# HGRN tile ends re-ordered, gathers paced, one FFN sum moved, and attention's value product as channel by token with probabilities divided first

## The chip, the cores and the metric

The kernel runs on one core of one Trainium2 chip. The metric is the device time of one execution in microseconds. TensorE is called PE (its weight loads PEld), VectorE DVE, ScalarE ACT, GpSimd POOL and SyncE SP; PEclk is the share of full clock that TensorE was granted.

## The reference

One decoder layer in float32 for a prompt of 1024 tokens and 8 sample tokens, D = 1024.

```
h1 = LN(alpha*x + 0.5*SwiGLU(x));  m = attention heads | HGRN2 heads, then w_out
h2 = LN(alpha*h1 + m);             y = LN(alpha*h2 + 0.5*SwiGLU(h2))
attention: indexer picks top 256 causal keys a query; p = softmax(q k / 8), o = p v
HGRN2:     S_t = diag(f_t) S_{t-1} + (1-f_t) i_t^T,  o_t = S_t^T q_t, RMS norm, silu gate
```

For the prompt, the selection is a mask added to the scores of all keys up to the query's block, so attention is dense in work: 8 query blocks of 128, 8 heads of 64 channels, 2 key/value heads. The sample rows gather their 256 selected keys and values from paged caches.

## The kernel before

All five engines have their own written-out program, and semaphores order them. The stages are FFN 1 (0 to 985 us of the span), projections, indexer and threshold search (to 1253), HGRN (to 1658), prompt attention (to 1902), the sample rows (to 1986), w_out (to 2118) and FFN 2 (to the end).

**FFN.** Each pair of hidden tiles is a Strassen-like scheme of seven products for gate and for up, in the order 1, 2, 6, 7, 5, 3, 4 (`up_pair`, matmuls at L1531). POOL forms the weight sums for gate, DVE those for up: `up_sums(0, p+1)` is three operations of 128x512 (L1870 to L1873) for the next pair. DVE multiplies product 3 into `h12` (L1891, `hidden`); that frees the PSUM bank in which the up half of the next pair's product 1 starts.

**HGRN.** Four tiles of two heads. A tile has eight level passes: DVE makes scaled operands (`level`, L1195 to L1200), PE multiplies the halves of all 8 blocks (`level_products`, L651), and DVE merges the PSUM result by mask (`mask`, L1213). A level's products need the banks that the mask of the level before has read. Between them DVE runs one bit of the sample rows' threshold search in each `sample_slot`: compare, count on PE (`count`, L606), fix the bit (L1088). Projection units (`unit`, L527 for 344 columns, L532 for 256) lie beside the levels by the table BESIDE; AFTER holds three more for the next tile, put into the tile's end. That end is, in order: tail keys (L1265), turned by PE (L674), copied by ACT (L913), update products (L682), eight state steps (L1220), output products (L692 with the masked matrix, L694 with the state, alternating), squares and root on ACT (L917, L919), and `outputs` on DVE (L1226 to L1236). `keep_top` (L1161 to L1167) turns a threshold into a mask.

**Attention.** 64 steps (block, head), from 8 key blocks down to 1. PE forms the scores of two heads (`qk_pair`, L711), DVE adds the mask and finds the maximum (`biggest`, L1293, L1295), ACT takes the exponential with its sum (L929), PE turns the probabilities (`turn_probs`, L722), ACT copies them (L938), and PE multiplies them by the values (`pv`, L732) to token by channel. After 8 heads DVE divides by the sums (L1302, L1303), PE turns the block (L741), and ACT stores it (L943). Meanwhile POOL issues 32 indirect gathers for the sample rows (L468) one after another. SP loads w_out by `mix(14..17)` into ring slots 2, 3, 0, 1.

Of the kernel before, what the change touches and what calls it, by code (L numbers as in the profile page):

```python
# [9 lines left out]
def build_decoder_step(nc, I, O):  # L10
# [10 lines left out]
    P = 128  # L21
# [23 lines left out]
    with ctx:  # L45
# [157 lines left out]
        def score(b):  # L203
# [31 lines left out]
        PT = TMP[:, 2048:4096].rearrange("p (u c) -> p u c", c=1024)  # L235
        OTOK = AUX[:, 0:1024].rearrange("p (u c) -> p u c", c=512)
# [25 lines left out]
        RSUM = SMALL[:, 120:128]  # L262
# [36 lines left out]
        at_qk, at_sm, at_exp, at_tr, at_ptc, at_pv, at_on, at_ott, at_otc = (sem("at_" + x) for x in (  # L299
            "logits", "max", "exp", "turned", "pt", "pv", "normed", "out_turned", "out_copied"))  # L300
# [25 lines left out]
        for beside, spread in ((row_units("rg", 0) + gate_units(1, 0), (1, 1, 2, 2, 2, 2, 1, 1)),  # L326
                               (gate_units(2, 0) + ri1[5:], (0, 1, 1, 1, 1, 1, 1, 1)),
                               (row_units("rg", 1) + gate_units(3, 0), (1, 1, 2, 2, 2, 2, 1, 1)), ([], (0,) * 8)):
            u, levels = len(UNITS), []
            for n in spread:  # L330
                levels.append(list(range(u, u + n)))
                u += n
            assert u == len(UNITS) + len(beside)
            UNITS += beside
            BESIDE.append(levels)
            AFTER.append(list(range(u, u + 3)) if beside else [])
            if beside:
                UNITS += gate_units(len(BESIDE), 1)
# [53 lines left out]
        def pool_mixer(pool, G, link):  # L392
# [16 lines left out]
            with nc_ok:  # L409
# [56 lines left out]
                for j in range(16):  # L466
                    for name, dst in (("cache_k", KS), ("cache_v", VS)):
# [20 lines left out]
                for slot in (2, 3, 0, 1):  # L488
# [22 lines left out]
        def pe_mixer(pe, cols, mean, var):  # L511
# [142 lines left out]
            for t in range(4):  # L654
                for lv in range(NPASS):
                    level_products(t, lv)
                    if (t, lv, 0) in DEC_SLOTS:
                        count(DEC_SLOTS.index((t, lv, 0)))
                    if t == 3:
# [6 lines left out]
                    for i, u in enumerate(BESIDE[t][lv]):  # L666
                        unit(u)
                        if i == 0 and (t, lv, 1) in DEC_SLOTS:
                            count(DEC_SLOTS.index((t, lv, 1)))
                pe.wait_ge(h_kt, t + 1)  # L670
                pe.wait_ge(h_at, 12 * (t + 1))
                pe.wait_ge(h_ax, 4 * (t + 1))
# [3 lines left out]
                for u in AFTER[t][0:1]:  # L676
                    unit(u)
                pe.wait_ge(h_ktok, t + 1)
                for c in range(BLK):
                    for hd in range(2):  # L680
                        rows = slice(64 * hd, 64 * hd + 64)
                        last = M(PS[rows, 6, HD * c:HD * c + HD], KTOK[:, c, rows], RI[:, c, P * t + HD * hd:P * t + HD * hd + HD],  # L682
                                 start=True, stop=True)
                last.then_inc(h_u, 1)
                for c in range(BLK):
                    if c:
                        pe.wait_ge(h_state, BLK * t + c)
                    for hd in range(2):
                        rows = slice(64 * hd, 64 * hd + 64)
                        out = PS[:, 4 + hd, HD * c:HD * c + HD]  # L690
                        e0 = P * t + HD * hd
                        last = M(out, AT[:, hd, c, :], RI[:, c, e0:e0 + HD], start=True, stop=c == 0)  # L692
                        if c:
# [22 lines left out]
            def turn_probs(i):  # L716
                b, _ = STEPS[i]
                pe.wait_ge(at_exp, i + 1)
# [6 lines left out]
            def pv(i):  # L725
                b, h = STEPS[i]
                pe.wait_ge(at_ptc, i + 1)
                if h == 0 and i:
                    pe.wait_ge(at_on, i // H)
                for j in range(b + 1):  # L730
                    c = P + HD * (h // 4)
                    last = M(PS[:, 2, HD * h:HD * h + HD], PT[:, i % 2, P * j:P * j + P], KV[:, j, c:c + HD],  # L732
                             start=j == 0, stop=j == b)
                last.then_inc(at_pv, 1)

            def turn_out_rows(bi):
                pe.wait_ge(at_on, bi + 1)
                if bi:
                    pe.wait_ge(at_otc, bi)
                for j in range(4):  # L740
                    last = T(PS[:, 3, P * j:P * j + P], OTOK[:, bi % 2, P * j:P * j + P], IDENT[:, :])  # L741
                last.then_inc(at_ott, 1)
# [9 lines left out]
            pv(63)  # L752
            turn_out_rows(7)


# [70 lines left out]
        def act_mixer(act, A, link, square, sd, gain):  # L826
# [79 lines left out]
            for t in range(4):  # L906
# [7 lines left out]
                for u in AFTER[t][0:1]:  # L914
                    unit(u)
                act.wait_ge(h_o, t + 1)
                A(OSQ.rearrange("p (u c) -> p u c", u=2), PS[:, 4:6, :], ACT.Square).then_inc(h_osq, 1)  # L917
                act.wait_ge(h_ss, t + 1)
                A(SR, SS, ACT.Sqrt, scale=1.0 / HD, bias=EPS[:, 2:3]).then_inc(h_sd, 1)  # L919
                for u in AFTER[t][1:3]:  # L920
                    unit(u)

            def expo(i):
                b, h = STEPS[i]
                act.wait_ge(at_sm, i + 1)
                if h == 0 and i >= 2 * H:
                    act.wait_ge(at_on, i // H - 1)
# [4 lines left out]
            def copy(i):  # L932
# [3 lines left out]
                if i >= 2:  # L936
                    act.wait_ge(at_pv, i - 1)
                A(PT[:, i % 2, 0:n], PS[:, 0:2, :].rearrange("p u c -> p (u c)")[:, 0:n], ACT.Copy).then_inc(at_ptc, 1)  # L938

# [1162 lines left out]
```

## Time and profile before

| what | us |
|---|---|
| median of 3 runs (lowest, highest) | 2991.72 (2990.32, 2992.75) |
| the profiled execution | 3020.13 |
| its span, first to last instruction | 3018.4 |
| mean granted clock | 0.934 |

The profiled execution is 28.4 us (0.95%) above the median; 1.7 us of its time lie outside the span. In a window's row the numbers in brackets are instruction counts. In a timeline the bracket at the end is the idle time of that engine before the instruction and who ended it; "issue" and "remote" are waits for which the profile shows no releaser. A float32 matmul appears as two PE instructions.

### The profile page before, as it was taken

To read this page: it belongs to the slowest core of one execution; us is meant where nothing else is said; L and a number is where in the kernel's file an instruction comes from. 1 tells how busy PE (TensorE), PEld (TensorE's weight loads), DVE (VectorE), ACT (ScalarE), POOL (GpSimd) and SP (SyncE) were. 2 spreads that over 40 slices of the span, in tenths; PEclk is the share of its full clock that TensorE was granted. 3 is DMA by queue.
4 is the path that set the end of the run, shared out by engine and by line. 5 is a ranking of instruction groups with operands and counts; after the bars stand their busy time and mean duration, and the time that the engine had idled before them with its cause. 6 is when DMAs were issued, how large, how long until landed. Compare 5 with 4: busy or idle time off the path is not lost.

```text
span 3018.4 us, 42478 instructions
## 1 busy us (share of the span) xinstructions
PE 2725.2 (90%) x17013; PEld 2440.3 (81%) x17013; DVE 1599.4 (53%) x3027; ACT 653.5 (22%) x1497; POOL 552.0 (18%) x534
## 2 busy tenths in 40 slices
PE   7999999999999799997996688398799999999996
PEld 7999999999987478875765566255799999999996
DVE  5654565365421878866668232413555455446543
ACT  1110221022011656410110344101221022102112
POOL 4321231133010111000000300212222132122300
PEclk9999999999999999988996787589899999999998
DMA  6473464346421233100100010101356246524632
GB/s 169 121 180 78 112 160 122 96 112 169 114 85 43 49 102 91 43 1 1 29 1 5 25 56 1 42 1 42 80 134 157 77 130 160 132 75 128 155 98 74
DMA packets 444179, 260.63 MB, mean 86 GB/s; under 512 B 8968, under 2 KB 436120, under 8 KB 443984
## 3 DMA queue, kind: packets, MB, share of 16 engines
q1 hardware_dynamic: 435712, 234.22, 29.5%
q0 software_dynamic: 8272, 23.70, 2.8%
q8 instruction: 136, 2.23, 0.3%
q14 instruction: 59, 0.48, 0.1%
HBM read 251.07 MB, written 6.81 MB: 85 GB/s over the span
## 4 chain that ended last, share of the span: by engine, by line
PE 63%; DVE 17%; issue 14%; ACT 3%; POOL 1%; SPq 1%; DMA 1%; DVEq 0%; POOLq 0%; ACTq 0%
PE ps L1531 22%; PE ps L1595 18%; PE ps L527 7%; PE ps L818 4%; PE ps L532 4%; DVE big L1870 3%; PE ps L651 2%; PE ps L592 2%; DVE big L1873 1%; DVE down_weights L1046 1%; PE ps L692 1%; PE ps L694 1%; DVE weight_ring L1887 1%; PE ps L583 1%; ACT acts L1713 1%
## 5 line engine op out<-in xcount | busy, mean ns | idle before, releaser
L1531 PE MATMUL ps<-aux,big 128*128 128x172 f32 x2112 | 339.5, 315 | 37.1 <-ACT big L1726 35.7
L1887 DVE TENSOR_TENSOR weight_ring<-ps,big 128x172 f32<-128x172 f32 x396 | 123.8, 331 | 440.9 <-ACT big L1726 393.3
L1531 PEld LDWEIGHTS ps<-aux,big 128*128 128x128 f32 x2112 | 320.7, 194 | 44.6 <-ACT big L1726 40.7
L1531 PE MATMUL ps<-acts,weight_ring 128*128 128x172 f32 x2112 | 333.2, 311 | 22.4 <-DVE weight_ring L1891 20.3
L1531 PEld LDWEIGHTS ps<-acts,weight_ring 128*128 128x128 f32 x2112 | 311.2, 190 | 37.1 <-issue 36.7
L1531 PE MATMUL ps<-weight_ring 128*128 128x172 f32 x2112 | 329.7, 309 | 0.0
L1531 PEld LDWEIGHTS ps<-weight_ring 128*128 128x128 f32 x2112 | 314.2, 190 | 0.0
L1595 PE MATMUL ps<-big 128*128 128x172 f32 x1584 | 238.8, 309 | 0.0
L527 PE MATMUL ps<-acts,weight_ring 128*128 128x344 f32 x768 | 238.2, 467 | 0.0
L1595 PEld LDWEIGHTS ps<-big 128*128 128x128 f32 x1584 | 233.1, 190 | 0.0
L2031 POOL TENSOR_TENSOR big<-weight_ring 128x512 f32<-128x512 f32 x66 | 83.8, 1269 | 726.6 <-PE ps L1531 702.9
L1726 ACT ACTIVATE big<-ps 128x172 f32<-128x172 f32 x396 | 119.4, 310 | 440.1 <-PE ps L1531 440.1
L527 PEld LDWEIGHTS ps<-acts,weight_ring 128*128 128x128 f32 x768 | 148.4, 197 | 73.9 <-issue 7.2
L532 PE MATMUL ps<-weight_ring,acts 128*128 128x256 f32 (+3 forms) x864 | 180.3, 364 | 0.0
L1730 ACT ACTIVATE weight_ring<-weight_ring 128x172 f32<-128x172 f32 x198 | 68.0, 344 | 478.3 <-DVE weight_ring L1887 478.2
L1531 PE MATMUL ps<-acts,big 128*128 128x172 f32 x1056 | 164.9, 309 | 0.0
L532 PEld LDWEIGHTS ps<-weight_ring,acts 128*128 128x128 f32 (+1 forms) x864 | 142.3, 180 | 25.9 <-issue 1.3
L1948 DVE SCALAR_TENSOR_TENSOR acts<-acts,ps 128x172 f32<-128x172 f32 x96 | 31.7, 330 | 247.3 <-PE ps L1595 247.3
L1595 PE MATMUL ps<-big,weight_ring 128*128 128x172 f32 x1056 | 159.9, 309 | 0.0
L1595 PE MATMUL ps<-big,down_weights 128*128 128x172 f32 x1056 | 159.9, 309 | 0.0
L1531 PEld LDWEIGHTS ps<-acts,big 128*128 128x128 f32 x1056 | 157.2, 190 | 0.0
L1595 PEld LDWEIGHTS ps<-big,down_weights 128*128 128x128 f32 x1056 | 155.6, 190 | 0.0
(335 smaller groups left out, 3932.1 us busy)
## 6 DMA issues: line engine op xcount, KB each, us to landing
weight_ring<-ffn_wg SPq DMA_DIRECT2D x132, 512.0 KB, 5.3
weight_ring<-ffn_wu SPq DMA_DIRECT2D x132, 512.0 KB, 7.0
down_weights<-ffn_wd SPq DMA_DIRECT2D x24, 1408.0 KB, 11.6
weight_ring<-ffn_wd SPq DMA_DIRECT2D x24, 1408.0 KB, 9.8
weight_ring<-w_in SPq DMA_DIRECT2D x9, 1024.0 KB, 5.3
weight_ring<-w_in SPq DMA_DIRECT2D x8, 512.0 KB, 7.2
weight_ring<-w_out SPq DMA_DIRECT2D x4, 1024.0 KB, 11.7
out_y_prompt<-weight_ring SPq DMA_DIRECT2D x8, 512.0 KB, 2.6
```

The costliest lines, as they stand in the source:

```text
L527: last = M(PS[:, u % 3, 0:TW], w[:, k, P * a:P * a + P], ACTS[:, k, cols(x)], start=k == 0, stop=k == DT - 1)
L532: last = M(PS[0:rows, u % 3, 0:a], ACTS[:, k, P * x:P * x + rows], w[:, k, :], start=k == 0, stop=k == DT - 1)
L592: last = M(PS[:, 5 + r % 2, 32 * j:32 * j + 32], KXT[:, r % 2, P * j:P * j + P], QB[:, :, :, 2 * gp:2 * gp + 2], start=True, stop=True)
L651: last = M(PS[:, 4 + 2 * half + hd, P * (c % 4):P * (c % 4) + P], k, q, start=True, stop=True)
L818: last = M(PS[:, y % 6, 0:TW], w[:, k, P * (d % 2):P * (d % 2) + P], src, start=k == 0, stop=k == DT - 1)
L1531: last = M(PS[:, 3 * m + bank, 0:QW], lhs[:, i, :], rhs[:, i, :], start=begin and i == 0, stop=end and i == KH - 1, skip_group_check=True)
L1595: last = M(PS[:, x + bank, 0:QW], lhs[:, i, :], rhs[:, i, :], start=begin and i == 0, stop=end and i == LAST, skip_group_check=True)
L1726: A(ST[:, m, c, :], PS[:, 3 * m, 0:QW], ACT.Copy).then_inc(cp_done, 1)
L1730: A(CG[:, i, :], CG[:, i, :], ACT.Silu).then_inc(sl_done, 1)
L1870: V.tensor_tensor(s1, a21, a22, ALU.add).then_inc(su_done[1], 1)
L1887: V.tensor_tensor((CG, CU)[m][:, (out, i)[m], :], PS[:, 3 * m + bank, 0:QW], ST[:, m, part, :], ALU.add)\
L2031: G.tensor_tensor(s1, a21, a22, ALU.add).then_inc(su_done[0], 1)
```

## The change

The diff does six things. FFN: `up_sums(0, p+1)` stands after `h12`. HGRN: BESIDE units go into the first six levels, AFTER units into levels 5 and 6; the counts stand ahead of the level's products and ahead of the units; the output products with the masked matrix run before the update products, into banks 6 and 7; `gates`, `queries` and the next tile's first `level` go ahead of `keep_top` and `outputs` on DVE, and the second half of the next tile's first products waits for `outputs`. Gathers wait for three attention steps a pair. Attention: every step's probabilities are divided ahead of turning (`normalise(i)`), and `pv_pair` multiplies values (stationary, 64 columns) by turned probabilities of two heads, so the result needs no turning. w_out loads in the order slot 0, 1, 2, 3, the last after attention.

```diff
-        for beside, spread in ((row_units("rg", 0) + gate_units(1, 0), (1, 1, 2, 2, 2, 2, 1, 1)),
-                               (gate_units(2, 0) + ri1[5:], (0, 1, 1, 1, 1, 1, 1, 1)),
-                               (row_units("rg", 1) + gate_units(3, 0), (1, 1, 2, 2, 2, 2, 1, 1)), ([], (0,) * 8)):
+        for beside, spread in ((row_units("rg", 0) + gate_units(1, 0), (2, 2, 2, 2, 2, 2, 0, 0)),
+                               (gate_units(2, 0) + ri1[5:], (1, 1, 1, 1, 1, 2, 0, 0)),
+                               (row_units("rg", 1) + gate_units(3, 0), (2, 2, 2, 2, 2, 2, 0, 0)), ([], (0,) * 8)):
...
                 for j in range(16):
+                    if j:
+                        pool.wait_ge(at_exp, 3 * j)
...
-                for slot in (2, 3, 0, 1):
+                for slot in range(4):
...
                     if t:
-                        pe.wait_ge(h_orow, t)
+                        pe.wait_ge(h_state, BLK * t)
...
+                    elif t and half:
+                        pe.wait_ge(h_orow, t)
...
-                    level_products(t, lv)
                     if (t, lv, 0) in DEC_SLOTS:
                         count(DEC_SLOTS.index((t, lv, 0)))
+                    level_products(t, lv)
+                    if (t, lv, 1) in DEC_SLOTS:
+                        count(DEC_SLOTS.index((t, lv, 1)))
...
+                    if lv == 5:
+                        for u in AFTER[t][0:1]:
+                            unit(u)
+                    elif lv == 6:
+                        for u in AFTER[t][1:3]:
+                            unit(u)
...
-                for u in AFTER[t][0:1]:
-                    unit(u)
+                pe.wait_ge(h_at, 12 * (t + 1))
+                pe.wait_ge(h_ax, 4 * (t + 1))
+                for c in range(BLK):
+                    for hd in range(2):
+                        e0 = P * t + HD * hd
+                        M(out(hd, c), AT[:, hd, c, :], RI[:, c, e0:e0 + HD], start=c == 0, stop=True, skip_group_check=True)
                 pe.wait_ge(h_ktok, t + 1)
...
+                for c in range(1, BLK):
+                    pe.wait_ge(h_state, BLK * t + c)
                     for hd in range(2):
-                        last = M(out, AT[:, hd, c, :], RI[:, c, e0:e0 + HD], start=True, stop=c == 0)
-                        if c:
-                            last = M(out, LV[rows, (t + 1) % 2, P * c:P * c + P], SC[rows, c, :], start=False, stop=True)
+                        last = M(out(hd, c), LV[rows, (t + 1) % 2, P * c:P * c + P], SC[rows, c, :],
+                                 start=False, stop=True, skip_group_check=True)
                 last.then_inc(h_o, 1)
-                for u in AFTER[t][1:3]:
-                    unit(u)
...
-                pe.wait_ge(at_exp, i + 1)
+                pe.wait_ge(at_sc, i + 1)
...
+            def pv_pair(q):
+                b, h = STEPS[2 * q]
+                bi = q // 4
+                pe.wait_ge(at_ptc, 2 * q + 2)
+                if q % 4 == 0 and bi >= 2:
+                    pe.wait_ge(at_otc, bi - 1)
+                c = P + HD * (h // 4)
                 for j in range(b + 1):
+                    for e in range(2):
+                        last = M(PS[64 * e:64 * e + 64, 2 + bi % 2, P * (q % 4):P * (q % 4) + P], KV[:, j, c:c + HD],
+                                 PT[(2 * q + e) % 4][:, P * j:P * j + P], start=j == 0, stop=j == b)
...
             for i in range(64):
                 turn_probs(i)
-                if i:
-                    pv(i - 1)
+                if i % 2 == 0 and i:
+                    pv_pair(i // 2 - 1)
                 if i % 2 == 0 and i + 2 < 64:
                     qk_pair(i // 2 + 1)
-                if i >= H and i % H == 2:
-                    turn_out_rows(i // H - 1)
...
             def queries(t):
+                V.tensor_copy(PF, HF[:, 0:SEQ]).then_inc(hf_free, 1)
...
+                if t < 3:
+                    gates(t + 1)
                 states(t)
                 if t < 3:
-                    gates(t + 1)
+                    queries(t + 1)
+                    level(t + 1, 1)
...
                 outputs(t)
-                if t < 3:
-                    queries(t + 1)
-                    level(t + 1, 1)
...
+            def normalise(i):
+                n = P * (STEPS[i][0] + 1)
+                dve.wait_ge(at_exp, i + 1)
+                r = RSUM[:, i % 2:i % 2 + 1]
+                link(V.reciprocal(r, SUMS[:, (i // H) % 2, i % H:i % H + 1]))
+                s = SM[:, i % 2, 0:n]
+                V.tensor_scalar(s, s, r, None, ALU.mult).then_inc(at_sc, 1)
+            biggest(0)
             for i in range(64):
-                biggest(i)
-                if i and i % H == 0:
-                    normalise(i // H - 1)
+                if i + 1 < 64:
+                    biggest(i + 1)
+                normalise(i)
...
+                elif m == 15:
+                    sp.wait_ge(at_pv, 32)
...
-                    for m in range(2, len(MIX)):
+                    for m in [*range(2, 14), 16, 17, 14, 15]:
...
-                if j < LAST:
-                    up_sums(0, p + 1)
                 dve.wait_ge(up_mm, up_count(p, 3, 1))
                 dve.wait_ge(sl_done, 4 * p + 3)
                 hidden(h12, h12, PS[:, 3, 0:QW])
+                if j < LAST:
+                    up_sums(0, p + 1)
```

PT now has four buffers, two of them in ring slot 3; `out_rows` copies the product's bank as it is.

## Rows read from the trace of the kernel before

**Rows 1.** The page's chain that ended last: share of the span by engine.
```profile
PE 63%; DVE 17%; issue 14%; ACT 3%; POOL 1%; SPq 1%; DMA 1%; DVEq 0%; POOLq 0%; ACTq 0%
```
**Rows 2.** Windows: length, busy time of PE, PEld, DVE, ACT, POOL, PEclk, DMA share, GB/s.
```profile
1253.00:1658.00 405.00, 340.46 (x2170) 268.75 (x2170) 282.49 (x538) 47.19 (x85) 10.61 (x13) 0.84 0.03 7
1365.00:1438.00 73.00, 53.43 (x366) 44.30 (x363) 54.30 (x105) 5.61 (x13) 0.00 (x0) 0.81 0.00 1
1658.00:1902.00 244.00, 194.20 (x1093) 153.41 (x1094) 78.63 (x234) 94.84 (x200) 28.79 (x30) 0.74 0.09 26
```
**Rows 3.** What L1531 waited for: us in total, times.
```profile
  DVE weight_ring L1891: 20.3, 59
```
**Rows 4.** Timeline of one FFN pair: start us, us, engine line, what, times [idle <-releaser].
```profile
321.59 1.75 DVE L1870 TENSOR_TENSOR big<-weight_ring 128x512 f32<-128x512 f32 x1
...
325.55 0.32 DVE L1891 TENSOR_TENSOR weight_ring<-weight_ring,ps 128x172 f32<-128x172 f32 x1
...
325.98 3.51 PEld L1531 LDWEIGHTS ps<-acts,weight_ring 128*128 128x128 f32 x24 [0.53 <-issue]
```
**Rows 5.** Waits from 1253 to 1658, DVE: us in total, times, longest.
```profile
DVE rejected L1088 <- PE ps L606: 34.4, 16, 4.0
```
**Rows 6.** Timeline of tile 0: one level's products; the tile's end.
```profile
1280.87 2.25 PE L651 MATMUL ps<-weight_ring 64*128 64x128 f32 x32 [1.40 <-DVE aux L1213]
...
1334.99 1.15 PE L682 MATMUL ps<-big,weight_ring 128*64 128x64 f32 x32
...
1352.10 11.52 PE L527 MATMUL ps<-acts,weight_ring 128*128 128x344 f32 x32
...
1364.37 2.06 PE L651 MATMUL ps<-big 64*128 64x128 f32 x32 [0.75 <-DVE down_weights L1182]
```
**Rows 7.** Timeline of tile 1's end on DVE: `keep_top`, then `outputs`.
```profile
1454.32 1.27 DVE L1161 TENSOR_SCALAR_CACHE_REDUCE big<-down_weights,candidate 128x1024 uint8<-128x1024 f32 x1
...
1455.63 0.75 DVE L1162 TENSOR_SCALAR weight_ring<-down_weights,candidate 128x1024 f32<-128x1024 f32 x1
...
1464.50 1.22 DVE L1226 TENSOR_REDUCE small<-weight_ring 128x16 f32<-128x1024 f32 x1 [2.23 <-ACT weight_ring L917]
1467.71 1.29 DVE L1236 TENSOR_TENSOR big<-big,ps 128x512 f32<-128x512 f32 x2
```
**Rows 8.** Timeline, attention with 1024 keys: `pv` at 0.5; then two steps at 1.0.
```profile
1702.19 3.52 PE L732 MATMUL ps<-big,weight_ring 128*128 128x64 f32 x16
...
1709.29 0.30 PEld L711 LDWEIGHTS ps<-big 64*128 64x128 f32 x4
1711.20 1.09 PE L722 MATMUL ps<-ident,weight_ring 128*128 128x128 f32 x8
...
1712.14 1.90 PE L732 MATMUL ps<-big,weight_ring 128*128 128x64 f32 x16
...
1712.69 1.23 DVE L1293 CUSTOM_DVE_ANT_0 weight_ring<-ps,down_weights 128x1024 f32<-128x1024 f32 x1
1713.96 0.15 DVE L1295 TENSOR_SCALAR small<-small 128x1 f32<-128x1 f32 x1
...
1717.78 1.77 PE L711 MATMUL ps<-big 64*128 64x512 f32 x8
```
**Rows 9.** Forms in attention: busy us, mean ns | idle before, releasers.
```profile
L1302 DVE RECIPROCAL small<-small 128x8 f32<-128x8 f32 x8 | 1.6, 203 | 27.2 <-PE ps L732 27.2
```
**Rows 10.** Timeline while the gathers run.
```profile
1677.37 1.02 ACT L938 ACTIVATE weight_ring<-ps 128x1024 f32<-128x1024 f32 x1 [4.27 <-remote]
...
1693.77 1.00 POOL L468 DMA_INDIRECT big<-cache_v,gather_rows  x1 [0.30 <-issue]
1698.54 1.02 ACT L938 ACTIVATE weight_ring<-ps 128x1024 f32<-128x1024 f32 x1 [18.36 <-remote]
```
**Rows 11.** Window of attention's last 50 us, columns as rows 2.
```profile
1850.00:1900.00 50.00, 43.77 (x186) 35.12 (x185) 13.49 (x66) 19.81 (x67) 0.00 (x0) 0.50 0.00 0
```
**Rows 12.** Timeline after attention: the path to the sample rows.
```profile
1915.50 3.50 DVE L1324 TENSOR_TENSOR down_weights<-big,down_weights 128x512 f32<-128x512 f32 x1 [15.09 <-DMA big<-scratch_ri]
```

More of the change, by code:

```diff
@@ L234, in build_decoder_step @@
         SM = TMP[:, 0:2048].rearrange("p (u c) -> p u c", c=1024)
-        PT = TMP[:, 2048:4096].rearrange("p (u c) -> p u c", c=1024)
-        OTOK = AUX[:, 0:1024].rearrange("p (u c) -> p u c", c=512)
+        PT = [TMP[:, 2048 + 1024 * i:3072 + 1024 * i] for i in range(2)] + [RING[:, 3, 1024 * i:1024 * i + 1024] for i in range(2)]
         KS = BIG[:, 2 * C4:2 * C4 + 2048].rearrange("p (j c) -> p j c", c=P)
@@ L261, in build_decoder_step @@
         SUMS = SMALL[:, 104:120].rearrange("p (u h) -> p u h", h=H)
-        RSUM = SMALL[:, 120:128]
+        RSUM = SMALL[:, 120:122]
         SS, SR = SMALL[:, 128:144], SMALL[:, 144:160]
@@ L298, in build_decoder_step @@
         kvout = sem("kv_out")
-        at_qk, at_sm, at_exp, at_tr, at_ptc, at_pv, at_on, at_ott, at_otc = (sem("at_" + x) for x in (
-            "logits", "max", "exp", "turned", "pt", "pv", "normed", "out_turned", "out_copied"))
+        at_qk, at_sm, at_exp, at_sc, at_tr, at_ptc, at_pv, at_otc = (sem("at_" + x) for x in (
+            "logits", "max", "exp", "normed", "turned", "pt", "pv", "out_copied"))
         qd_zero, qd_in, vn_in, s0_in, vb_in = sem("qd_zeroed"), sem("qd_in"), sem("vn_in"), sem("s0_in"), sem("vb_in")
@@ L665, in pe_mixer @@
                             select_c(lv - 4)
-                    for i, u in enumerate(BESIDE[t][lv]):
+                    for u in BESIDE[t][lv]:
                         unit(u)
-                        if i == 0 and (t, lv, 1) in DEC_SLOTS:
-                            count(DEC_SLOTS.index((t, lv, 1)))
+                    if lv == 5:
[4 more added lines that the diff above has]
+                            unit(u)
                 pe.wait_ge(h_kt, t + 1)
-                pe.wait_ge(h_at, 12 * (t + 1))
-                pe.wait_ge(h_ax, 4 * (t + 1))
+                pe.wait_ge(h_ax, 4 * t + 3)
                 for c in range(BLK):
@@ L681, in pe_mixer @@
                         rows = slice(64 * hd, 64 * hd + 64)
-                        last = M(PS[rows, 6, HD * c:HD * c + HD], KTOK[:, c, rows], RI[:, c, P * t + HD * hd:P * t + HD * hd + HD],
+                        last = M(PS[rows, 4, HD * c:HD * c + HD], KTOK[:, c, rows], RI[:, c, P * t + HD * hd:P * t + HD * hd + HD],
                                  start=True, stop=True)
                 last.then_inc(h_u, 1)
-                for c in range(BLK):
-                    if c:
-                        pe.wait_ge(h_state, BLK * t + c)
+                for c in range(1, BLK):
+                    pe.wait_ge(h_state, BLK * t + c)
                     for hd in range(2):
                         rows = slice(64 * hd, 64 * hd + 64)
-                        out = PS[:, 4 + hd, HD * c:HD * c + HD]
-                        e0 = P * t + HD * hd
-                        last = M(out, AT[:, hd, c, :], RI[:, c, e0:e0 + HD], start=True, stop=c == 0)
-                        if c:
-                            last = M(out, LV[rows, (t + 1) % 2, P * c:P * c + P], SC[rows, c, :], start=False, stop=True)
+                        last = M(out(hd, c), LV[rows, (t + 1) % 2, P * c:P * c + P], SC[rows, c, :],
+                                 start=False, stop=True, skip_group_check=True)
                 last.then_inc(h_o, 1)
-                for u in AFTER[t][1:3]:
-                    unit(u)
             pe.wait_ge(h_orow, 4)
@@ L913, in act_mixer @@
                 A(KTOK[:, :, :].rearrange("p (u c) x -> p u (c x)", u=2), PS[:, 4:6, :], ACT.Copy).then_inc(h_ktok, 1)
-                for u in AFTER[t][0:1]:
+                for u in AFTER[t]:
                     unit(u)
                 act.wait_ge(h_o, t + 1)
-                A(OSQ.rearrange("p (u c) -> p u c", u=2), PS[:, 4:6, :], ACT.Square).then_inc(h_osq, 1)
+                A(OSQ.rearrange("p (u c) -> p u c", u=2), PS[:, 6:8, :], ACT.Square).then_inc(h_osq, 1)
                 act.wait_ge(h_ss, t + 1)
                 A(SR, SS, ACT.Sqrt, scale=1.0 / HD, bias=EPS[:, 2:3]).then_inc(h_sd, 1)
-                for u in AFTER[t][1:3]:
-                    unit(u)
             def expo(i):
@@ L925, in expo @@
                 act.wait_ge(at_sm, i + 1)
-                if h == 0 and i >= 2 * H:
-                    act.wait_ge(at_on, i // H - 1)
+                if i >= 2 * H:
+                    act.wait_ge(at_sc, i - 2 * H + 1)
                 s = SM[:, i % 2, 0:P * (b + 1)]
@@ L948, in act_mixer @@
                 copy(i)
-                if i >= H and i % H == 2:
+                if i >= H and i % H == 1:
                     out_rows(i // H - 1)
@@ L1235, in outputs @@
                 for hd in range(2):
-                    last = V.tensor_tensor(rg[:, hd], rg[:, hd], PS[:, 4 + hd, :].rearrange("p (c e) -> p c e", e=HD), ALU.mult)
+                    last = V.tensor_tensor(rg[:, hd], rg[:, hd], PS[:, 6 + hd, :].rearrange("p (c e) -> p c e", e=HD), ALU.mult)
                 last.then_inc(h_orow, 1)
```

46 lines of the change are left out of this document (11 added, 35 removed).

## The prediction

> **What bounds the kernel now.** I read the chain that ended last, then windows by stage, then waits and timelines at the six places that the diff touches. PE carries 63% of the chain and DVE 17% [rows 1]. In both FFNs PE is the bound, so what counts there is its idle time. HGRN and attention are hand-offs between PE and DVE: HGRN's 405 us hold 340 of PE and 282 of DVE, attention's 244 hold 194 and 79 [rows 2]. Their clock is 0.84 and 0.74 of full, so the level granted matters as much as the instruction count. The reader should see that PE's 194 busy microseconds in attention are no proof that PE work sets its length.
>
> The sum goes by the profiled execution, 3020.13 us, 28.4 above the median of 2991.72. I carry the difference over unchanged and treat the one place where that is doubtful (the gathers) apart.
>
> **FFN: up_sums behind h12.** PE waits for L1891 59 times [rows 3]. In the timeline the three sums begin at 321.59, h12 ends only at 325.87, and PE's load resumes at 325.98 after 0.53 us idle [rows 4]. With h12 first it is done about 0.35 us after product 3, some 3 us before its bank is needed, so the wait goes: 59 x 0.55 = **-32 us**. What is late next? The sums start about 0.8 us later, at 322.4, and with 4.0 us (325.55 - 321.59) end near 326.4; their reader, product 6 of the next pair, stands behind the 24 loads that end at 329.5 (325.98 + 3.51). The addition and SiLU behind them slip 0.6 us, with over 1 us to spare. Bounds: 0, if another engine is late at once, and -35.
>
> **HGRN.** Per tile the mixed output products run from 1336.14, the end of L682, to 1352.10: 16.0 us [rows 6]. Apart they are 32 instructions like L732's, 1.90/16 = 0.12 us each [rows 8], 3.8 us, and 28 of 64 columns, at most 0.11 each by L651's 2.25/32 = 0.07 and what is left for waits on the states, 3.1 us. That is 9 less a tile, 36 in all. Here the row is first: one block's share is 16.0/8 = 2.0 us for seven or eight instructions of 0.12. [...]
>
> The counts ahead of the level's products take from DVE's 34.4 us of waiting [rows 5]. In tiles 0 and 2, with two units beside each level, PE becomes the bound, and the second count now holds the units until DVE's compare; I take 11 of the 34.
>
> Against this stands a new wait. The second half of the next tile's first products waits for `outputs`, and PE has nothing behind it that may pass. On DVE stand before that: queries and a level (3.7 us, six operations of about 0.65), `keep_top` (1464.50 - 2.23 - 1454.32 = 8.0 us, not in tile 0), and `outputs` with its ACT steps (1464.50 to 1469.00, 4.5 us) [rows 7]. PE idles 8 + 16 + 15 = 39 us in three tile ends, where before it had units: 11.5 us of L527 directly behind the outputs [rows 6]. The units are not gone but moved into the levels, where only tile 1 has room: 73.0 - 53.4 = 20 us idle [rows 2], of which I let 12 take them up. Sum: -36 - 11 + 39 - 12 = **-20 us**; bounds -40 (the idle covered) and +10 (units make all levels longer).
>
> **Attention, the chain of a pair.** Before, with 1024 keys at full clock, a pair of heads takes 1717.78 - 1709.29 = 8.49 us [rows 8]. On PE it is two turnings of 0.86 (1.09 with the drain), two value products of 1.87 and the scores of 1.8: 7.3 of 8.5, mostly hidden behind DVE and ACT and they behind it. After the change the order in the code is a strict alternation: `biggest(2q+2)` needs the scores; `normalise(2q+1)` stands behind it on DVE; turning 2q+1 needs that; `biggest(2q+3)` needs this turning (its buffer); then `normalise(2q+2)`, turning 2q+2, `pv_pair`, and the next scores. Prices: `biggest` 1712.69 to 1714.11 = 1.42; `normalise` a reciprocal of 0.20 [rows 9] and a scaling like L1162's 0.75 of the same 1024 columns [rows 7], 1.0 with the gap; turnings 1.09 and 0.86; `pv_pair` has no row. Bounds: it has 32 instructions of 128 columns, of pairs on different column halves. L651's pairs of row halves with the same 128 columns take 0.07 each; L682's pairs of column halves with 64 columns 1.15/32 = 0.036 [rows 6]; alone they would take L732's 0.12. So 1.7 to 3.8 us; I take 2.0, next to L682, which is the same layout. Sum: 2 x 1.42 + 2 x 1.0 + 1.09 + 0.86 + 2.0 + 1.8 + four hand-offs of 0.05 = 10.8 us, **2.3 more than before**, although PE lost 1.7 us of work. Most pieces shrink with the key blocks; I let the difference fall evenly to 0.2 at one block, a mean of 1.25, times 32 pairs: +40. Off go the division at the block ends (27.2 us of DVE waits in eight [rows 9], of which 11 are on the chain, as the pair around a block end is some 3 longer while scores fill all four banks), `keep_top` now beside more PE work (-3) and the last division and turning (-2). [...] At an equal clock: **+27 us**.
>
> **Attention, the clock.** PE's needed time falls to 5.6 of 10.8 us. [...] `pv` at the lower level took 3.52 instead of 1.90 [rows 8]. If all pairs of three or more key blocks ran low, each would lose its PE pieces once more: 5.6 us at eight blocks, 2.1 at three, a mean of 3.9 over 24, 93 us. I take **+26**: three tenths more of the time low than before. Bounds 0 and +65. [...]
>
> **Gathers.** From 1673.1 to 1677.4 and from 1680.2 to 1698.5 ACT stood still with all it needed done, and moved 4 us after the last gather was issued [rows 10]: 22.6 us, 19 net of the value products that crept along. Three steps (some 13 us) between pairs of gathers leave room, and the last pair, after step 45, is early enough for the sample rows. But the profiled execution is above the timed ones by about this much (28.4 us), so whether those stall too is open. I take half: **-10 us**; bounds 0 and -22.
>
> **w_out and the tail.** Slot 3 holds probabilities until the end and loads only then, 1 MB beside the state loads that DVE waits for until 1915.50 [rows 12]: **+1 us**, bounds 0 and +6. The wait at POOL's scaling has 70 us of cover.
>
> **Sum.** -32 - 20 + 27 + 26 - 10 + 1 = -8 us: 3012 for a profiled execution, **2984 us** for the median. 0.2% (6 us) is what a measurement of this kernel tells from no change.
>
> **The rivals.**
> 1. Recovery: the stall is real in timed runs and the clock no worse. -32 - 20 + 27 + 3 - 19 + 1 = -40: 2952 us. For it: the standstill with all inputs ready. Against: PE's thinner work.
> [...]
> 3. The value pairs do not run side by side: 3.8 instead of 2.0 us at eight blocks, 32 us over all: 3016 us. Against: L682's 0.036.
> 4. The FFN gap stays, because another engine is late (the change doesn't do what it says): 3016 us. Against: only pairs with the sums ahead show it.
>
> **How the numbers follow.** Forecast 0.40 (2966 to 3000), rival 1 0.22, rival 2 0.24, rivals 3 and 4 0.07 each. The range is 2946 to 3026. Faster by over 0.2% (under 2985.7): 0.24 of the forecast, 0.22 of rival 1, 0.01 of the rest: 0.47. Within: 0.15. Slower: 0.38.
>
> **What would show it.** In the FFN: no wait for L1891. In HGRN: the masked products in one run of about 4 us; an idle of 8 to 16 us before the second half of the first products of tiles 1 to 3. In attention: pairs of 10.8 us at full clock with 1024 keys, the scaling following `biggest`, PEclk under 0.74, no standstill at the start. Wrong it is if pairs stay at 8.5 us or if attention's clock rises.

## The result, and the profile after

The changed kernel took 3021.87 us (median of 4, 3020.73 to 3023.45) against 2991.02 us for the kernel before (median of 4, 2989.20 to 2992.75): a ratio of 1.0104, 95% interval 1.0086 to 1.0121. It is 30.9 us, or 1.0%, slower. The forecast was 2984 us, a little faster than before; 3021.87 lies inside the range given, but the time moved the other way. The rival nearest to it is the second, which has 60 us for the lower clock in attention and nothing at the gathers: -32 - 20 + 27 + 60 + 1 = +36, 3028 us.

The profiled executions differ by 2 us only (3020.13 before, 3022.25 after). That is because the one of before stands still at the gathers [rows 10] and its timed runs in this comparison are 29 us shorter, which suggests that they did not. In the changed kernel the profiled execution and the timed median lie 0.4 us apart. The experiments come back to that.

The chain that ended last, after, beside rows 1: "issue" fell from 14% to 6%, and PE now has 74%.

```profile
PE 74%; DVE 16%; issue 6%; ACT 2%; DMA 1%; SPq 1%; POOL 1%; DVEq 0%; ACTq 0%; POOLq 0%
```

Windows of HGRN, of attention, and of attention's last 50 us, after (columns as in rows 2):

```profile
1245.00:1624.00 379.00, 290.49 (x2172) 234.62 (x2172) 282.14 (x533) 46.06 (x84) 8.84 (x11) 0.88 0.04 13
1624.00:1913.00 289.00, 178.32 (x1058) 118.23 (x1059) 110.49 (x346) 100.47 (x200) 30.96 (x31) 0.69 0.04 11
1863.00:1913.00 50.00, 29.54 (x139) 16.07 (x140) 17.11 (x90) 17.88 (x58) 0.00 (x0) 0.50 0.00 1
```

HGRN was 405 us [rows 2] and is 379. Attention was 244, of which 22.6 were the standstill [rows 10], and is 289: 45 us longer although it no longer stands still. DVE's time in it rose from 79 to 110 us, and the granted clock fell from 0.74 to 0.69. PE's 178.3 and DVE's 110.5 us add up to 288.8 of the 289: the two hardly ever work at the same time.

What PE waited for, in us, times and longest wait, over the whole span, after:

```profile
PE ps L731 <- DVE weight_ring L1302: 110.3, 63, 3.9
PE ps L1530 <- ACT big L1725: 39.1, 18, 11.7
PE ps L654 <- DVE big L1235: 32.0, 3, 13.9
...
PE ps L654 <- DVE aux L1212: 18.6, 8, 5.5
```

The first row is the new one in attention: 63 of the 64 turnings wait for the scaling (L1302), 1.75 us each. The third is the new one in HGRN, three tile ends, as predicted. The wait of the FFN's products for h12 [rows 3] has no row any more. One FFN pair, after (start us, us, engine, line): h12 is the first line, the sums for the next pair begin behind it at 317.80.

```profile
317.54 0.33 DVE L1890 TENSOR_TENSOR weight_ring<-weight_ring,ps 128x172 f32<-128x172 f32 x1 [0.58 <-PE ps L1530]
317.80 0.85 DVE L1869 TENSOR_TENSOR big<-weight_ring 128x512 f32<-128x512 f32 x1
...
319.82 4.68 PE L1530 MATMUL ps<-acts,weight_ring 128*128 128x172 f32 x31
```

PE runs through where rows 4 show its loads resuming at 325.98 after h12. The end of HGRN's tile 0, after, to hold against rows 6:

```profile
1331.75 3.69 PE L692 MATMUL ps<-big,aux 128*128 128x64 f32 x32
...
1336.90 2.34 PE L704 MATMUL ps<-big,weight_ring 64*128 64x64 f32 x28 [0.39 <-DVE big L1219]
...
1340.05 1.16 PE L654 MATMUL ps<-big 64*128 64x128 f32 x16 [0.81 <-DVE down_weights L1181]
...
1347.12 2.08 PE L654 MATMUL ps<-big 64*128 64x128 f32 x16 [5.90 <-DVE big L1235]
```

The masked products take 3.69 us in one run and the state products 2.34, together 6.0 where the mixed loop took 16.0. Then PE does half of the next tile's first products and waits 5.90 us for `outputs`.

The trace of before shows what the mixed loop was made of. PE alternates between two instructions of L692 and two of L694, with no wait for a state among them. In tile 0 such a group starts every 0.36 us at first, and every 0.62 us from 1339.15 on, where the granted clock is 0.50 although PE's records fill the window (the second excerpt, columns as in rows 2):

```profile
1337.33 0.43 PE L692 MATMUL ps<-big,aux 128*128 128x64 f32 x2
1337.70 0.43 PE L694 MATMUL ps<-big,weight_ring 64*128 64x64 f32 x2
...
1339.77 0.69 PE L692 MATMUL ps<-big,aux 128*128 128x64 f32 x2
1340.38 0.69 PE L694 MATMUL ps<-big,weight_ring 64*128 64x64 f32 x2
```

```profile
1339.00:1352.00 13.00, 13.00 (x44) 10.56 (x43) 2.17 (x5) 0.00 (x0) 0.68 (x1) 0.50 0.01 3
```

The four tiles took 16.0, 14.0, 15.0 and 15.9 us. With all 27 alternations at the full clock each would be 10.7 us (an estimate: 0.87 for the first six instructions and 27 x 0.364). So about half of what the new order saves is the alternation itself (10.7 - 6.0 = 4.7 us a tile) and half is the lower clock that went with it (15.2 - 10.7 = 4.5, with the mean of the four).

The same view of one pair of heads in attention, 1024 keys, after. It is the central piece of the result:

```profile
1664.22 1.23 DVE L1292 CUSTOM_DVE_ANT_0 weight_ring<-ps,down_weights 128x1024 f32<-128x1024 f32 x1 [2.32 <-PE ps L720]
...
1665.75 0.75 DVE L1302 TENSOR_SCALAR weight_ring<-weight_ring,small 128x1024 f32<-128x1024 f32 x1
...
1666.56 1.09 PE L731 MATMUL ps<-ident,weight_ring 128*128 128x128 f32 x8 [2.47 <-DVE weight_ring L1302]
...
1667.80 1.23 DVE L1292 CUSTOM_DVE_ANT_0 weight_ring<-ps,down_weights 128x1024 f32<-128x1024 f32 x1 [1.30 <-PE ps L731]
...
1670.14 1.97 PE L731 MATMUL ps<-ident,weight_ring 128*128 128x128 f32 x8 [2.48 <-DVE weight_ring L1302]
...
1672.04 3.68 PE L743 MATMUL ps<-weight_ring,big 128*64 128x128 f32 x32
...
1675.64 1.89 PE L720 MATMUL ps<-big 64*128 64x512 f32 x8
...
1677.57 1.09 DVE L1292 CUSTOM_DVE_ANT_0 weight_ring<-ps,down_weights 128x896 f32<-128x896 f32 x1 [7.49 <-PE ps L720]
```

The reader is to see a relay: `biggest`, scaling, turning, `biggest`, scaling, turning, value products, scores, and then `biggest` again after 7.49 us of waiting, with PE and DVE never beside each other. The order is the one that the prediction read from the code. It takes 13.35 us (1664.22 to 1677.57) where before it took 8.49 [rows 8]. PE's pieces come at two speeds: the first turning takes 1.09 us with 1.0 granted, the second 1.97 and the value products 3.68 with 0.5 granted.

### The profile page after: what moved, and what is told of

Read it like the earlier page. It is cut to its first block, busy times and chain, and to the rows that moved or that the text cites. A ratio compares the mean times of both kernels' runs of the same rounds, so it can differ in the third digit from the quotient of the medians.

```text
span 3020.4 us, 42557 instructions
## 1 busy us (share of the span) xinstructions
PE 2654.6 (88%) x16981; PEld 2381.9 (79%) x16981; DVE 1581.1 (52%) x3139; ACT 657.5 (22%) x1497; POOL 550.7 (18%) x534
## 4 chain that ended last, share of the span: by engine, by line
PE 74%; DVE 16%; issue 6%; ACT 2%; DMA 1%; SPq 1%; POOL 1%; DVEq 0%; ACTq 0%; POOLq 0%
PE ps L1530 29%; PE ps L1594 18%; PE ps L528 7%; PE ps L533 5%; PE ps L818 4%; PE ps L731 2%; PE ps L593 2%; PE ps L743 2%; PE ps L720 1%; DVE weight_ring L1292 1%; DVE down_weights L1044 1%; PE ps L584 1%; ACT acts L1712 1%; DVE weight_ring L1302 1%; PE ps L654 1%
## 5 line engine op out<-in xcount | busy, mean ns | idle before, releaser
L1530 PE MATMUL ps<-aux,big 128*128 128x172 f32 x2112 | 346.8, 319 | 42.5 <-ACT big L1725 39.1
L1530 PEld LDWEIGHTS ps<-aux,big 128*128 128x128 f32 x2112 | 326.8, 197 | 49.7 <-ACT big L1725 44.1
L1530 PE MATMUL ps<-acts,weight_ring 128*128 128x172 f32 x2112 | 319.2, 309 | 1.7 <-DVE acts L1816 0.9
L528 PE MATMUL ps<-acts,weight_ring 128*128 128x344 f32 x768 | 231.7, 458 | 0.0
L731 PE MATMUL ps<-ident,weight_ring 128*128 128x128 f32 x288 | 66.2, 378 | 110.3 <-DVE weight_ring L1302 110.3
```

The costliest lines, as they stand in the source:

```text
L528: last = M(PS[:, u % 3, 0:TW], w[:, k, P * a:P * a + P], ACTS[:, k, cols(x)], start=k == 0, stop=k == DT - 1)
L731: last = T(PS[:, j // 4, P * (j % 4):P * (j % 4) + P], SM[:, i % 2, P * j:P * j + P], IDENT[:, :])
L1530: last = M(PS[:, 3 * m + bank, 0:QW], lhs[:, i, :], rhs[:, i, :], start=begin and i == 0, stop=end and i == KH - 1, skip_group_check=True)
```

## The experiments

The kernel before did not stand still on every occasion. Kernels timed on the same occasion share its runs, so each comparison below has its own figure for it: 3014.49 us (3001.09 to 3020.81), 3014.83 (3003.30 to 3020.03), 2987.17 (2985.41 to 2990.42) and 3013.00 (2997.53 to 3021.04).

**e_ffn**: the kernel before with the FFN's edit alone, the last hunk of the diff.

> The kernel before with the FFN edit alone (up_sums behind h12), against 2991.0 us of before. Theory A (the gap is worth what PE itself idles, 0.30 us as PE's row has it, not the 0.53 of the loads' row; 58 pairs): -17 us, 2974. Theory B (the prediction's 0.55 us a pair): -32 us, 2959. If another engine is late at once: 2991.

Measured: 2995.61 us against 3014.49, ratio 0.9935 (0.9912 to 0.9958): -18.9 us (-13 to -27). The size is theory A's; the absolute time is not, because the kernel before stood at 3014. Between the two traces 6.1 of the 21.9 us lie in attention's first seven blocks (216.3 us, 222.3 before), whose code is the same in both, and 15.8 outside them.

**e_hgrn**: the HGRN edits alone (the spreads, the counts ahead of the products, the split output products, the bank change, gates and level moved).

> The kernel before with the HGRN edits alone. Theory A (the stage's 404 us in the trace of before and 379 in the trace of after is what the edits do): -25 us, 2966, with two to three idles of 6 to 14 us before the second half of the next tile's first products. Prediction: -20, 2971. Rival: the stage gains but the attention behind it starts at a lower clock and gives half of it back: 2979.

Measured: 2983.43 us, 0.9898 (0.9878 to 0.9919): -31.1 us. More than any of the three; e_ffnhgrn and h_again below come back to it.

**e_gather**: the wait ahead of each pair of gathers alone.

```
                 for j in range(16):
+                    if j:
+                        pool.wait_ge(at_exp, 3 * j)
```

> The kernel before with the paced gathers alone. Theory A (the standstill of 22.6 us is of the profiled execution only, which is 28 us above the timed ones): timed 2991 +- 3, its profiled execution about 2995 to 3000. Theory B (the timed runs stall too): 2970, profiled 2998.

Measured: 2992.62 us (2984.15 to 2999.55), 0.993 (0.9906 to 0.9955): -21.9 us. In the timeline of ACT in e_ffn, whose gathers are issued in one go, the standstill is there; it is the idle in brackets:

```profile
1674.13 1.02 ACT L938 ACTIVATE weight_ring<-ps 128x1024 f32<-128x1024 f32 x1 [7.45 <-remote]
...
1693.35 1.02 ACT L938 ACTIVATE weight_ring<-ps 128x1024 f32<-128x1024 f32 x1 [16.41 <-remote]
```

23.9 us in all. What ACT waited for in e_gather over the same stretch has no such row, and the copy (L940 there) waits 0.7:

```profile
ACT weight_ring L931 <- DVE small L1297: 26.8, 6, 7.1
ACT weight_ring L940 <- PE ps L724: 0.7, 1, 0.7
```

So the standstill is the gathers', and timed runs can have it (theory B on this occasion). It is seen in the profiled executions; for the timed ones it is inferred from the medians.

**e_noattn**: the three parts together, with the old attention and the old order of the w_out loads.

> The kernel before with the FFN, HGRN and gather edits and the old attention (and the old order of the w_out loads). Theory A (parts add): 2991 - 17 - 25 = 2949, and the attention part alone then costs 3022 - 2949 = +73 us. Rival (the parts interact, as the clock of one stage depends on the one before): 2960 to 2975.

Measured: 2944.36 us (2943.84 to 2945.94), 0.9773 (0.9750 to 0.9795). The three single gains sum to -71.8 us and this is -70.1: they add. Against the changed kernel it leaves 77.5 us for the attention part, the order of the w_out loads included, which was not tried alone.

**a_again**: the changed kernel once more.

> The changed kernel once more, to stand beside the kernel before where that runs 3001 to 3021 us. Theory A (the standstill at the gathers comes and goes with the occasion, in whole sets of runs, and only kernels that issue the gathers in one go have it): 3022 here too, however before stands. Rival (the occasion shifts all kernels alike): 3045.

Measured: 3021.65 us (12 runs, 3020.03 to 3023.79) against 3014.83, 1.0026 (1.0013 to 1.0039). Theory A: the changed kernel is where it was to 0.2 us, and the kernel before is 24 us up. The loss is 31 us where the kernel before runs free and 7 us where it stands still.

**e_swap**: the changed kernel with two statements of PE's loop exchanged.

```
+                if i % 2 == 0 and i + 2 < 64:
+                    qk_pair(i // 2 + 1)
                 if i % 2 == 0 and i:
                     pv_pair(i // 2 - 1)
-                if i % 2 == 0 and i + 2 < 64:
-                    qk_pair(i // 2 + 1)
```

> The changed kernel with the next pair's scores issued ahead of the pair's value products. Theory S (series: the value products stand between the turning and the next scores and DVE waits for both; 1.9 to 3.7 us a pair with 1024 keys, a mean of about 1.5): -48 us, 2974. Rival C (clock: DVE's and PE's alternation leaves PE too thin; the order within PE's stretch changes nothing in that): at most the half of it, 2998 and a clock in attention no higher.

Measured: 2960.34 us (2957.58 to 2963.30), 61.3 under a_again. More than theory S gave, and the clock rose, against C (0.78 in attention, 222 us instead of 289). The timeline shows what it does: scores (3.36 us at the lower clock, 0.50, where they took 1.89), then values, and DVE starts beside the values:

```profile
1665.33 1.97 PE L731 MATMUL ps<-ident,weight_ring 128*128 128x128 f32 x8 [2.48 <-DVE weight_ring L1302]
...
1667.23 3.36 PE L720 MATMUL ps<-big 64*128 64x512 f32 x8
...
1670.52 1.73 PE L743 MATMUL ps<-weight_ring,big 128*64 128x128 f32 x26
1670.62 1.09 DVE L1292 CUSTOM_DVE_ANT_0 weight_ring<-ps,down_weights 128x896 f32<-128x896 f32 x1 [5.34 <-PE ps L720]
```

**e_fill**: the changed kernel with work on PE whose result nobody reads, in the time in which it waits for the scaling.

```
-                pe.wait_ge(at_sc, i + 1)
                 if i:
                     pe.wait_ge(at_ptc, i)
+                for j in range(b + 1):
+                    T(PS[:, 0, 0:P], IDENT[:, :], IDENT[:, :])
+                pe.wait_ge(at_sc, i + 1)
```

> The changed kernel with idle work on PE: before each turning, once its bank is free and while the scaling is awaited, as many further turnings of the identity as there are key blocks. Theory C (at least 40 of the 76 us that attention lost are PE at the lower level because it idles): granted clock in attention from 0.69 to 0.85 or more, 2982 us. Theory S (the series is what costs; clock little): the clock may rise, the time stays at 3015 to 3030.

Measured: 2986.48 us (2985.48 to 2988.41): 35.2 us faster for 288 more instructions, with the clock in attention at 0.87 and its length 248 us. Theory C, though the gain is some 5 us short of the 40 that it named. The pair with 1024 keys, now at full clock throughout (1.00 from 1657.48 to 1668.12):

```profile
1657.48 1.23 DVE L1294 CUSTOM_DVE_ANT_0 weight_ring<-ps,down_weights 128x1024 f32<-128x1024 f32 x1 [0.74 <-PE ps L720]
...
1664.42 1.97 PE L745 MATMUL ps<-weight_ring,big 128*64 128x128 f32 x32
...
1668.12 1.09 DVE L1294 CUSTOM_DVE_ANT_0 weight_ring<-ps,down_weights 128x896 f32<-128x896 f32 x1 [4.78 <-PE ps L720]
```

10.64 us from one `biggest` to the next pair's (1668.12 - 1657.48), where the prediction had 10.8; the value products 1.97, where it had 2.0.

**e_nodiv**: the changed kernel without the scaling; the attention output is left undivided.

> The changed kernel without the scaling of the probabilities (the attention output is left undivided; the reciprocal stays). Theory S (the scaling of 0.75 us with 1024 keys, a mean of 0.52, stands in series 64 times): -35 us, 2987. Rival (PE is the bound and the scaling hides): 3020. If the clock rises with PE's idle time gone: down to 2970.

Measured: 2963.65 us (2954.39 to 2967.53), 58.0 under a_again, for a group of 33.3 us of DVE work. Its clock in attention is 0.77 instead of 0.69: with a piece of DVE work gone from the relay PE is without work for 75 of 231 us instead of 111 of 289, its clock is higher, and the gain is larger than the piece. The runs spread over 13 us, so the size is rough.

**e_swapfill** and **e_swapfill5**: both edits together; in the second, at least five idle turnings.

> The changed kernel with both the scores ahead of the value products (which gave -61 us alone) and the idle work ahead of each turning (-35 alone). If the two costs are separate (series and clock) and the order took only part of the clock's share: attention from 222 us to about 205, 2943. If the order already took what the idle work gives: 2960, or more where the idle work now delays PE.

> As the run before, with at least five idle turnings ahead of each (only pairs of four key blocks or fewer differ). If the lower clock of the last three blocks (0.50 to 0.82) is due to PE's idle time there: 5 to 10 us under that run. If the extra work lies in the way: 5 us above it.

Measured: 2942.33 us (2936.24 to 2945.95) and 2939.20 (2936.80 to 2939.65). The first is as expected if the costs are separate. The second is 3.1 us under it; its clock in the last query block, of one key block, is 1.00 where the first's is 0.73, but the ranges overlap.

**e_oldfill**: the old attention, otherwise as e_noattn, with the same idle turnings.

> The old attention with the FFN, HGRN and gather edits (2944 us) and the same idle work ahead of its turnings. Where PE at the lower level costs as much there as in the changed attention: 2925. As its turnings wait only 25 us for the exponential and its clock in attention is 0.86 already: at most -8, 2936 to 2944, and above 2944 if the idle work delays the turnings.

Measured: 2952.17 us (2951.31 to 2952.93), 7.8 above e_noattn (of another occasion) though its clock rose from 0.86 to 0.91. There the idle work lies in the way.

**e_ffnhgrn**: FFN and HGRN edits, gathers as before.

> The kernel before with the FFN and HGRN edits and the gathers as they were. If the gathers in one go cost 22 us whatever the rest: 2966, with a standstill of about 22 us in its trace. If the HGRN and FFN gains were partly the standstill shortened: 2950.

Measured: 2948.46 us (2946.12 to 2951.79), 0.9866 (0.9851 to 0.9881), against a kernel before of 2987.17. Neither expectation fits its own reason: nobody stood still on this occasion, the kernel before included, and this one's trace has no such wait. FFN and HGRN are worth 38.7 us there; with e_ffn's 18.9, which is from another occasion, that leaves 19.8 for HGRN.

**best**, **n_again**, **e_fill12**, **h_again**: the kernel of e_swapfill5, that of e_noattn and that of e_hgrn once more, and the changed kernel with twelve and eight idle turnings at every block.

> The whole change with the scores ahead of the value products and at least five idle turnings ahead of each turning. It gave 2939.2 beside another occasion's 2944.4 of the old attention. Theory (at a full clock the two attentions are level: 204 us here, 210 there): 2937 to 2941, 3 to 7 us under n_again.

> The FFN, HGRN and gather edits with the old attention once more: 2944, as before, whatever the occasion, since its gathers are paced.

> The changed kernel with more idle work: twelve idle turnings ahead of each even one and eight ahead of each odd one, at every block. If with e_fill's 0.87 clock there were still some 15 us to be had: clock in attention 0.95 or more, 2970 us, so that the clock costs about 50 of the 77 us and the series about 27. If the rest is series: 2986 or, with the idle work in the way at few key blocks, up to 3000.

> The kernel before with the HGRN edits alone, once more. If this occasion's kernel before runs without the standstill (2987 to 2991): -20 to -25 us, 2966 to 2970. If it stands still again: -31, 2983, and the five microseconds above come from a shorter standstill.

Measured: 2938.15 us (2936.41 to 2940.47), 2943.67 (2942.23 to 2946.28), 2983.04 (2982.57 to 2983.84) and 2981.03 (2980.35 to 2982.69). Attention in the first three, one window each, in the order e_fill12, n_again, best:

```profile
1628.00:1872.00 244.00, 198.59 (x1698) 152.14 (x1697) 110.22 (x346) 101.41 (x202) 31.47 (x32) 0.98 0.05 14
```

```profile
1625.00:1835.00 210.00, 168.89 (x1086) 134.68 (x1087) 78.47 (x234) 94.75 (x201) 30.77 (x32) 0.86 0.10 30
```

```profile
1625.00:1829.00 204.00, 165.77 (x1422) 117.52 (x1422) 110.56 (x346) 100.73 (x200) 31.43 (x31) 0.99 0.05 16
```

At 0.98 the changed attention still takes 244 us against the old one's 210 at 0.86. So of the 78.0 us between the changed kernel and n_again, the idle work brings back 38.6 (3021.65 - 2983.04) with the clock, and 39.4 stay: 34 in attention, 3 ahead of it and 2 behind. It falls between the two expectations of e_fill12.

That is no comparison at an equal clock, since the old attention is at 0.86. Other traces have single blocks of the same code at the full clock. The query block of four key blocks (four pairs of heads) in n_again and in e_gather, then three key blocks in n_again and in e_oldfill (idle work included), columns as in rows 2:

```profile
1753.72:1777.95 24.23, 19.66 (x122) 15.41 (x123) 7.56 (x27) 11.09 (x25) 5.87 (x6) 0.86 0.05 14
```

```profile
1794.44:1815.59 21.15, 16.58 (x122) 13.08 (x123) 7.56 (x27) 10.98 (x25) 5.87 (x6) 1.00 0.06 16
```

```profile
1777.95:1800.85 22.90, 20.03 (x98) 15.75 (x99) 6.52 (x26) 9.40 (x25) 4.64 (x6) 0.67 0.05 15
```

```profile
1787.92:1806.96 19.04, 15.96 (x123) 13.15 (x124) 6.52 (x27) 9.37 (x25) 4.55 (x5) 1.00 0.07 19
```

So n_again itself loses at least 7 us to the clock (3.1 and 3.9). At an equal clock the changed attention is then about 40 us longer than the old one and not 34, and about 32 of the 38.6 are what it loses to the clock beyond the old one. Both are estimates: the idle work may itself delay the blocks with few keys (four key blocks take 28.13 us in e_fill12 and 26.75 in e_fill, both at 1.00).

**best** beats the changed kernel by 83 us, the kernel before by 2.4% (ratio 0.9761, 0.9739 to 0.9784) where that stands still, and the old attention of n_again by 5.5 us, with ranges that do not meet. Against a kernel before that runs free the same kernel, as e_swapfill5, is 1.6% faster (0.9835, 0.9822 to 0.9849).

h_again stood still again (its first eight steps' stretch is 20 us longer than n_again's), as did the kernel before it was compared with. So its -32 us do not come from a shorter standstill, against what was expected. The attention behind the standstill took 173 us there and 183 in e_gather, two kernels with the same attention code (the kernel before's profiled execution has 182 from its ninth step on):

```profile
1691.00:1864.00 173.00, 139.54 (x899) 112.92 (x898) 62.23 (x202) 77.91 (x177) 0.00 (x0) 0.85 0.08 25
```

```profile
1693.00:1876.00 183.00, 152.93 (x904) 124.00 (x903) 62.37 (x202) 78.18 (x178) 26.78 (x28) 0.77 0.11 33
```

DVE and ACT do the same (62 and 78 us), PE's clock is 0.85 and 0.77. That is 9 to 10 of the 12 us between h_again and HGRN's 19.8. It does not go with the HGRN edits alone: e_ffn has the old HGRN, and its blocks of seven to two key blocks take 156.7 us as in h_again, against 164.8 in e_gather. What sets the level in one and not in the other was not tested.

## Why the prediction was wrong, point by point

- **FFN, -32 forecast, -18.9 measured.** The mechanism was right, the wait is gone. The mis-sized term is "59 x 0.55 = **-32 us**". It took the 0.53 us of idle time of PE's weight loads [rows 4] for PE's own; rows 3 had the total for PE's matmuls, 20.3 us in 59 times, 0.34 each. In e_ffn two other waits of PE grew, the ones for ACT L1726 from 35.7 to 38.7 us and for DVE L1832 from 28.4 to 29.9: 20.3 - 4.5 = 15.8. Of the fourth rival only these 4.5 us came true.
- **HGRN, -20 forecast, -19.8 measured** on an occasion without standstill, and -25 between the traces. The total is right, its terms less so. The output products save 37 us in the four tiles where 36 was said, but the 16.0 us of tile 0 were the longest of the four, and about half of the saving is the lower clock that the alternation ran at (0.50), which the prediction does not count. The new idle is 32.0 us in three tile ends (5.9, 13.9 and 12.2) where 39 was. The counts did not give 11: DVE's wait for them is 38.9 us in twelve (L1086) against 34.4 in sixteen [rows 5]. What makes up for it is the level's shorter wait (PE for DVE, 41.0 us before and 18.6 after). That the total fits so well is partly luck.
- **Attention at an equal clock, +27 forecast, about +40 measured** (at least +34, e_fill12 against n_again). This is the first step that failed. The order and the pair's 10.8 us at 1024 keys were right (10.64). What failed is "I let the difference fall evenly to 0.2 at one block". From a block's first `biggest` to the next block's, e_fill12 is 4.7, 3.9, 9.0, 5.6, 3.9, 1.4 and 3.6 us longer than n_again for eight to two key blocks, and 7.0 and 5.3 for four and three by the rows at the full clock. The forecast, with its 13 us of savings spread evenly, has 7.6, 6.4, 5.2, 4.0, 2.8, 1.6 and 0.4: too much for many keys, too little for few. Why the loss does not shrink with the keys was not tested. The terms named come to 40 - 11 - 3 - 2 = 24; the other 3 of the 27 are a guess of 0.1 us a pair for one more change between shapes of product, which no run shows. What the traces show of such changes is HGRN's: alternating, two instructions start every 0.364 us at the full clock, where in runs of their own two take 0.23 (3.69/16) and 0.17 (2.34/14).
- **Attention's clock, +26 forecast, about +32 measured** (at most +39). The direction was right and the size short. The clock records of the traces have two levels, 0.50 and 1.00, and the share of time at the lower one was right: (1 - 0.69)/0.5 = 0.62 after, 0.28 in n_again, three tenths more. But the prediction started from the 0.74 of the trace of before, which is 0.52 with a standstill in it (PE is busy for 8.0 of its 22.6 us); that the step upward came out at three tenths is luck. That more work on PE can raise its clock is what e_fill shows: 0.69 to 0.87, and 35.2 us.
- **Gathers, -10 forecast.** The step was a half between two cases, and both exist: -21.9 where the kernel before stands still, and little where it runs free, as it seems to have done in the result's timed runs (e_ffnhgrn and n_again differ by the pacing alone and by 4.8 us, on different occasions). The 28.4 us between the profiled and the timed execution, which the sum carried over unchanged, are 0.4 in the changed kernel.
- **The tail, +1 forecast.** Outside attention e_fill12 and n_again differ by 5 us, 3 ahead of it and 2 behind; the bound of +6 holds.

With the runs in place of the terms: -19 - 20 + 34 + 39 + 0 + 5 = +39, against +31 measured. The 8 us over are differences between occasions and the gathers: 3.9 between the two free medians of the kernel before (2991.02 and 2987.17) and 4.8 between e_ffnhgrn and n_again. Against the forecast of -8 the largest miss is attention, 73 us in its two terms where 53 was said; those 20 us alone turn the sign. The FFN's 13 come next. The cause is the relay and its lower clock, as the second rival's sum has it, but with about 32 us of clock in place of its 60, and about 40 at an equal clock in place of 27. That its +36 came so near is partly chance, since it also had 32 for the FFN.

## What to carry to other kernels

Write the loop of two engines out as a relay before pricing it. If each piece waits for the one before, moving work from PE to DVE can cost twice, as it did here: in length (some 40 us), and in PE's clock (some 32), which was 0.86 with PE idle for 41 of 210 us (n_again) and 0.69 with 111 of 289 (the changed kernel). The order of two statements (scores ahead of values) alone was worth 61 us, as much as the FFN, HGRN and gather edits together (19, 20 and 22). Price a PE wait by PE's own matmul row: 0.34 us a time here, where the weight loads' row had 0.53 and 15.8 us came back in 59 times. A gain in one stage may be partly clock, as about half of the 37 us of HGRN's output products was, by the estimate above: look at the granted clock on both sides before it is put down to an order of instructions. And a standstill in the one profiled execution has to be looked for in the spread of the timed runs, over several occasions, before it is counted as gain or as none.

## What the runs showed of the hardware

- Work without a use made a kernel faster: 288 idle turnings in attention brought -35.2 us and 0.69 to 0.87 of granted clock (e_fill). In the old attention, at 0.86 to begin with, the same edit cost 7.8 us (e_oldfill).
- PE's records can fill a window while the granted clock is 0.50: 13.0 of 13.0 us in HGRN's mixed output products, where full-array and half-row instructions alternated two by two. The same products in two runs took 3.69 and 2.34 us at 1.00.
- Taking 33.3 us of DVE work out of the relay (e_nodiv) gave 58.0 us, with the clock in attention at 0.77 instead of 0.69.
- The kernel before, whose indirect gathers are issued in one go, seems to stand still on some occasions only: medians of 2991.0 and 2987.2 us on two, 3014.5, 3014.8 and 3013.0 on three. With the gathers spread over attention the repeated kernels stayed within about 1 us (2944.36 and 2943.67; 3021.87 and 3021.65; 2939.20 and 2938.15). On one of the free occasions a kernel that issues them in one go (e_ffnhgrn) has no such wait in its trace. What makes an occasion one or the other stayed open.
